# The first feed-forward fed from unscaled, turned rows, with the norm's root applied to every product tile

## The reference, cut to what matters

```python
x = x + rms_norm(merged @ w_out, norm_g[1])
h = rms_norm(x, norm_g[2])
gt, up = jnp.split(h @ w_ffn_in, 2, axis=-1)
x = x + rms_norm((jax.nn.silu(gt) * up) @ w_ffn_out, norm_g[3])
```

## Time and profile before

| | |
|---|---|
| median of 3 runs | 2281.73 us (2281.44 to 2281.91) |
| profiled execution, its own time | 2282.81 us |
| its span | 2281.0 us |
| PE busy, share of the span | 98% |
| DVE, ACT, POOL busy | 64%, 41%, 12% |
| mean granted clock of PE | 0.995 |
| DMA | 358 MB, 157 GB/s |

### The profile page before, as it was taken

One profiled execution on the slowest core, in us unless ns is written; L12 is line 12 of the kernel. 1 busy time (PEld: TensorE's weight loads), 2 busy tenths in 40 slices (PEclk: granted clock), 3 DMA queues, 4 the chain that ended last, 5 costly groups with the idle time before them and its releaser, 6 DMA issues.

```text
span 2281.0 us, 33428 instructions
## 1 busy us (share of the span) xinstructions
PE 2246.4 (98%) x14230; PEld 1963.7 (86%) x14230; DVE 1455.3 (64%) x1953; ACT 927.2 (41%) x1332; POOL 281.9 (12%) x254
## 2 busy tenths in 40 slices
PE   8999999999999999999999999999999999999999
PEld 8999986989998888888769888888888888988999
DVE  7675557777768767757858676326755332887554
ACT  7854447454562122235554212124322212556443
POOL 2020105111101011000110201000100101202111
PEclk9999989999999999999999999999999999999999
DMA  7453451746545444423204444223453321623443
GB/s 292 185 203 148 146 219 41 270 185 258 195 144 217 171 198 190 170 83 130 79 24 162 175 194 185 74 93 140 156 221 152 143 94 73 175 103 111 185 185 111
DMA packets 35728, 358.23 MB, mean 157 GB/s; under 512 B 4237, under 2 KB 6477, under 8 KB 9212
## 3 DMA queue, kind: packets, MB, share of 16 engines
q1 hardware_dynamic: 32124, 343.54, 39.6%
q0 software_dynamic: 3456, 12.56, 2.0%
HBM read 353.11 MB, written 1.13 MB: 155 GB/s over the span
## 4 chain that ended last, share of the span: by engine, by line
PE 93%; DVE 3%; ACT 2%; issue 1%; DMA 0%; SPq 0%; POOLq 0%; ACTq 0%; DVEq 0%
PE psum L931 25%; PE psum L932 25%; PE psum L933 25%; PE psum L1013 2%; PE psum L1012 2%; PE psum L1011 2%; PE psum L1324 1%; PE psum L952 1%; PE psum L947 1%; PE psum L948 1%; PE psum L1298 1%; PE psum L1253 1%; PE psum L1268 1%; DVE small L2798 0%; ACT arena_r L1631 0%
## 5 line engine op out<-in xcount | busy, mean ns | idle before, releaser
L931 PE MATMUL psum<-arena_r 128*128 128x256 f32 (+1 forms) x3096 | 1046.2, 338 | 5.2 <-DVE arena_r L2544 3.2
L933 PE MATMUL psum<-arena_r,ring_r 128*128 128x256 f32 (+1 forms) x3096 | 1039.8, 336 | 0.0
L932 PE MATMUL psum<-zT_r,arena_r 128*128 128x256 f32 (+1 forms) x2336 | 774.9, 332 | 0.0
L1631 ACT ACTIVATE arena_r<-ring 128x2048 fp32r<-128x2048 f32 (+1 forms) x252 | 473.4, 1880 | 691.0 <-PE psum L933 639.1
L2243 DVE TENSOR_TENSOR ring_r<-ring,arena_r 128x2048 fp32r<-128x2048 f32 (+1 forms) x252 | 572.3, 2273 | 192.5 <-ACT arena_r L1631 191.8
L931 PEld LDWEIGHTS psum<-arena_r 128*128 128x128 f32 x3096 | 583.8, 189 | 81.7 <-issue 4.7
L933 PEld LDWEIGHTS psum<-arena_r,ring_r 128*128 128x128 f32 x3096 | 586.4, 189 | 65.3
L932 PEld LDWEIGHTS psum<-zT_r,arena_r 128*128 128x128 f32 x2336 | 440.0, 188 | 43.8
L932 PE MATMUL psum<-arena_r 128*128 128x256 f32 (+2 forms) x1208 | 396.8, 328 | 0.0
L2399 DVE CUSTOM_DVE_ANT_0 psum<-arena,cb 128x1024 f32<-128x1024 f32 x256 | 318.0, 1301 | 0.0
L932 PEld LDWEIGHTS psum<-arena_r 128*128 128x128 f32 x1208 | 228.3, 189 | 22.1
(11 more groups left out here) (366 smaller groups left out, 2370.5 us busy)
## 6 DMA issues: line engine op xcount, KB each, us to landing
ring<-in_wf SPq DMA_DIRECT2D x75, 2048.0 KB, 7.5
ring<-in_w SPq DMA_DIRECT2D x40, 2048.0 KB, 7.6
arena<-in_w SPq DMA_DIRECT2D x73, 1024.0 KB, 9.4
ring<-in_wf SPq DMA_DIRECT2D x10, 1536.0 KB, 6.3
ring<-in_w SPq DMA_DIRECT2D x6, 1024.0 KB, 8.8
arena<-strip_scratch POOLq DMA_DIRECT2D x1, 2048.0 KB, 11.6
arena<-rpb_scratch POOLq DMA_DIRECT2D x16, 128.0 KB, 10.8
xT<-in_x SPq DMA_DIRECT2D x1, 1024.0 KB, 7.2
```

The lines of the kernel that those rows point to most:

```text
L931: mm(b[c][:, at], whc, xh[:, k, at], start=(k == ks[0]), stop=False)
L932: mm(b[c][:, at], whc, xl[:, k, at], start=False, stop=False)
L933: last = mm(b[c][:, at], wlc, xh[:, k, at], start=False, stop=(k == ks[-1]))
L1631: A(W_hi[h % NHI][:, 0:n], ring[:, half_slot(h)], ACT.Identity).then_inc(sig("w_hi"), 1)
```

## The change

It takes out the scaled tokens: the hi and lo parts are made of the turned x times the norm's weights, straight from PSUM, and the root is multiplied into both product tiles of every input half. So:

- **Border, by token tile.** DVE: sum, root, reciprocal and row additions of tile 0, then of tile 1 (`tile_rows`), each with its own root on ACT (`tile_root`); the weight rest that stood ahead of them is cut in two, one half ahead and one behind (`w_lo_part`). PE turns tile 0's rows, then tile 1's (`turn_rows_by_tile`). ACT squares the rows (`tile_squares`) and then writes the eight hi parts from PSUM (`raw_hi`); DVE writes the rests from PSUM (`raw_low`). The copies `x_back(0, ..)`, the scalings and the old parts are gone. The matmul that spreads the root moves in between the first half's matmuls, ahead of k = 3 (`raw_ready`), and ACT copies it to `R_root`.
- **Every input half of ffn 0.** DVE multiplies both tiles by `R_root` into `R_t` (`raw_half`) and signals with an empty instruction; ACT applies Silu in place (`raw_silu`); DVE multiplies gate and up (`raw_gate`, one half later, and the last of a group in the first output half); `a_high` also waits for that. Both tiles are now emptied by DVE.

The diff, cut to its core:

```diff
@@ make_plan @@
-                      "VV" if f == 4 and c == 0 else "AV")
+                      "VV" if f == 0 or f == 4 and c == 0 else "AV")
...
-    add("norm2", None, "V")
+    add("norm2", None, "A")
@@ tensor @@
+            def raw_ready(k):
+                pe.wait_ge(sig("raw_lo"), k + 1)
+                if k == 3:
+                    b = open_tile(TILE["norm2"])
+                    pe.wait_ge(sig("x_diag"), 1)
+                    mm(b[:, 0:S], C("ones"), rr[:, 0:2 * P], start=True, stop=True).then_inc(filled, 1)
...
+                    elif f == 0 and not second:
+                        split_part(h, half_banks(h), slice(0, S), R_hi, R_lo, filled,
+                                   before=raw_ready if i == 0 else None, both=i == 0)
...
-            turn_rows(0)
-            b = open_tile(TILE["norm2"])
-            pe.wait_ge(sig("x_diag"), 1)
-            mm(b[:, 0:S], C("ones"), rr[:, 0:2 * P], start=True, stop=True).then_inc(filled, 1)
+            turn_rows_by_tile()
@@ scalar @@
                     w_hi(h + 2)
+                    if f == 0 and not second:
+                        raw_silu(GROUPS[g][0] + j)
+                        if j > 0:
+                            a_high(g, j - 1)
...
+            def raw_silu(m):
+                act.wait_ge(sig("raw_t"), m + 1)
+                t = R_t[m % 2][:, 0, :]
+                A(t, t, ACT.Silu).then_inc(sig("raw_silu"), 1)
...
             evac_pairs("w_out", 4, w_out)
-            row_roots(0)
-            z_high(2, 0, 0, 2)
-            x_back(0, 3)
-            z_high(2, 0, 2, KT)
+            tile_squares()
+            raw_hi(0)
+            raw_hi(1)
+            act.wait_ge(sig("tok_sum"), 3)
+            A(X_RT, X_TOT, ACT.Sqrt, scale=1.0 / D, bias=C("eps")).then_inc(sig("tok_rt"), 1)
+            for k in range(2, KT):
+                raw_hi(k)
+            b = empty(TILE["norm2"])
+            A(R_root, b[:, 0:S], ACT.Identity).then_inc(evac["A"], 1)
@@ vector @@
+                    if f == 0 and second and j == 0:
+                        raw_gate(GROUPS[g][0] + GROUPS[g][1] - 1, GROUPS[g][1] - 1)
                     w_lo(h + 2)
+                    if f == 0 and not second:
+                        raw_half(m, n)
+                        if j > 0:
+                            raw_gate(m - 1, j - 1)
...
+            def raw_half(m, n):
+                if m == 0:
+                    wait_evac(dve, TILE["norm2"])
+                for i in range(2):
+                    b = empty(n + i)
+                    last = v.tensor_tensor(out=R_t[m % 2][:, i, :], in0=b[:, 0:S], in1=R_root, op=ALU.mult)
+                    last.then_inc(evac["V"], 1)
+                dve.engine_nop().then_inc(sig("raw_t"), 1)
+
+            def raw_gate(m, j):
+                dve.wait_ge(sig("raw_silu"), m + 1)
+                if m >= 2:
+                    dve.wait_ge(sig("a_lo"), m - 1)
+                t = R_t[m % 2]
+                v.tensor_tensor(out=(rt, rr)[j % 2][:, 0:S], in0=t[:, 1, :], in1=t[:, 0, :], op=ALU.mult)\
+                    .then_inc(sig("raw_gate"), 1)
...
+            gained(2, 0)
+            gained(2, 1)
+            w_lo_part(HALF_AT["w_out3"] + 2, 0)
             dve.wait_ge(sig("x_tok_in"), 16)
+            tile_rows(0, lambda: gained(3, 0))
+            tile_rows(1, lambda: gained(3, 1))
+            w_lo_part(HALF_AT["w_out3"] + 2, 1)
+            dve.wait_ge(sig("norm_sq"), 3 * KT)
+            v.tensor_reduce(out=X_TOT, in_=X_SUM.rearrange("p (t c) -> p t c", t=2), axis=AX, op=ALU.add)\
+                .then_inc(sig("tok_sum"), 1)
+            raw_low(0)
+            raw_low(1)
```

More of the change, by code:

```diff
@@ L967, in tail, with turn_rows_by_tile @@
                 split_part(h + 1, [high_bank(n + 2), high_bank(n + 3)], c_, xh, xl, filled, ks=ks)
+            def turn_rows_by_tile():
+                for t in range(2):
+                    for c in range(4):
+                        pe.wait_ge(sig("norm_x"), 4 * t + (2 if c < 2 else 4))
+                        for i in range(2):
+                            at = (4 + c) * BANK + i * S + t * P
+                            last = nc.tensor.transpose(psum[:, at:at + P], X_row[:, 4 * t + c, i * P:(i + 1) * P],
+                                                       C("ident"))
+                        if t == 1:
+                            last.then_inc(sig("x_turned"), 1)
             def turn_rows(n):
@@ L1055, in ffn @@
                     before = None
-                    if i == (2 if f == 4 else 0):
+                    if f == 4 and i == 2:
                         before = split_ready(NORM_BEFORE[f], 0)
@@ L1066, in ffn @@
                     else:
-                        split_features(h, nt, *((hi, lo) if second else (z_hi(nt), z_lo)), before=before,
-                                       both=i == (2 if f == 4 else 0))
+                        split_features(h, nt, *((hi, lo) if second else (z_hi(nt), z_lo)), before=before)
                     if f == 0 and i == CTX_TOTAL:
@@ L1772, in x_back, with tile_root, tile_squares, raw_hi @@
                   ACT.Identity).then_inc(sig("x_back"), 1)
+            def tile_root(t):
+                act.wait_ge(sig("tok_sum"), t + 1)
+                A(O_RT[:, t:t + 1], O_TOT[:, t:t + 1], ACT.Sqrt, scale=1.0 / D, bias=C("eps")).then_inc(sig("tok_rt"), 1)
+            def tile_squares():
+                for t in range(2):
+                    for h in range(2):
+                        k = 4 * t + 2 * h
+                        act.wait_ge(sig("norm_x"), k + 2)
+                        A(zT[:, k:k + 2, 0:S], X_row[:, k:k + 2, :], ACT.Square,
+                          accum_out=X_SUM[:, 2 * t + h:2 * t + h + 1]).then_inc(sig("norm_sq"), 2)
+            def raw_hi(k):
+                act.wait_ge(sig("x_turned"), k // 2 + 1)
+                A(R_hi[:, k, :], x_bank(k), ACT.Identity, scale=V("norm_g", 16 + k, 1)).then_inc(sig("raw_hi"), 1)
+            def raw_silu(m):
+                act.wait_ge(sig("raw_t"), m + 1)
+                t = R_t[m % 2][:, 0, :]
+                A(t, t, ACT.Silu).then_inc(sig("raw_silu"), 1)
             def row_roots(n):
-                act.wait_ge(sig("tok_sum"), 2 * n + 1)
+                act.wait_ge(sig("tok_sum"), 2 * n + 2)
                 A(O_RT, O_TOT, ACT.Sqrt, scale=1.0 / D, bias=C("eps")).then_inc(sig("tok_rt"), 1)
@@ L2490, in gained_out, with w_lo_part @@
                                        in1=G_row[3][:, c * S:(c + 1) * S], op=ALU.mult)
+            def w_lo_part(h, s):
+                n = HALVES[h][2] // 2
+                at = half_slot(h).start + s * n
+                if s == 0:
+                    assert h == lo_made[0]
+                    dve.wait_ge(sig("w_hi"), h + 1)
+                low = v.tensor_tensor(out=ring_r[:, at:at + n], in0=ring[:, at:at + n],
+                                      in1=W_hi[h % NHI][:, s * n:(s + 1) * n].bitcast(f32), op=ALU.subtract)
+                if s == 1:
+                    lo_made[0] += 1
+                    low.then_inc(sig("w_lo"), 1)
@@ new lines, in raw_low @@
+            def raw_low(k):
+                dve.wait_ge(sig("raw_hi"), 2 * (k // 2) + 2)
+                v.scalar_tensor_tensor(out=R_lo[:, k, :], in0=x_bank(k), scalar=V("norm_g", 16 + k, 1),
+                                       in1=R_hi[:, k, :].bitcast(f32), op0=ALU.mult, op1=ALU.subtract)\
+                    .then_inc(sig("raw_lo"), 1)
+            def raw_half(m, n):
+                if m == 0:
+                    wait_evac(dve, TILE["norm2"])
+                for i in range(2):
+                    b = empty(n + i)
+                    last = v.tensor_tensor(out=R_t[m % 2][:, i, :], in0=b[:, 0:S], in1=R_root, op=ALU.mult)
+                    last.then_inc(evac["V"], 1)
+                dve.engine_nop().then_inc(sig("raw_t"), 1)
@@ new lines, in raw_gate, with tile_rows @@
+            def raw_gate(m, j):
[5 more added lines that the diff above has]
+                    .then_inc(sig("raw_gate"), 1)
+            def tile_rows(t, between):
+                dve.wait_ge(sig("norm_sq"), KT + 7 + t)
+                v.tensor_reduce(out=O_TOT[:, t:t + 1], in_=O_SUM[:, 4 * t:4 * t + 4], axis=AX, op=ALU.add)\
+                    .then_inc(sig("tok_sum"), 1)
+                link(between())
+                dve.wait_ge(sig("tok_rt"), t + 1)
+                link(v.reciprocal(O_RR[:, t:t + 1], O_RT[:, t:t + 1]))
+                for h in range(2):
+                    k = slice(4 * t + 2 * h, 4 * t + 2 * h + 2)
+                    v.scalar_tensor_tensor(out=X_row[:, k, :], in0=Y_y[:, k, :], scalar=O_RR[:, t:t + 1],
+                                           in1=xT[:, k, 0:S], op0=ALU.mult, op1=ALU.add).then_inc(sig("norm_x"), 2)
@@ L2918, in _ @@
             dve.wait_ge(sig("g_row_in"), 2 * 16)
-            for c in range(4):
+            for c in range(3):
                 lo(f"w_out{c}")
@@ L2925, in _ @@
                     gained(c - 1, 1)
[L2926 removed]
```

(14 more changed lines are left out.)

41 lines of the change are left out of this document (19 added, 22 removed).

## The result

| | before | after |
|---|---|---|
| median | 2281.59 us (2278.72 to 2282.80, 6 runs) | 2291.78 us (2287.98 to 2294.72, 6 runs) |
| profiled execution, own time and span | 2282.81, 2281.0 | 2294.01, 2292.2 |
| ratio to before | | 1.005 (95% interval 1.004 to 1.006) |

The change makes the kernel slower by 10.2 us in the medians (9 to 14 by the interval). 2293 was forecast.

What follows compares the result with a forecast made beforehand. The prediction took PE, busy for 98% of the span, as the bound. Feed-forward waits of 13.75 us less 2.7 us gained at the border, +11.1 on the 2281.73 us median, made 2293 us; 8-in-10 range 2286 to 2300.

Steps and rivals of the forecast that it cites:

- The ring: First feed-forward's input halves: split, DVE work, Silu and copy wait in a loop, 5.7 us a round against PE's 5.65.
- lag of a set of dots: Input halves: four adaptation reduces on DVE delay the emptying of a half's tiles by 2.9 us per set.
- Waits per group: First feed-forward: PE waits 3.75, 8.75 and 1.25 us in groups 0, 1 and 2, 13.75 us together.
- lag - 1.55: PE's wait per group, early waits for empty tiles included: the accumulated delay less 1.55 us of slack.
- POOL's last subtraction: At each group's end, ahead of the first output half: taken at 1.1 us, some 1 us lower sum if short.
- The border: Output projection to first feed-forward: first matmul 3.9 us earlier, less 1.2 for the root's matmuls, a gain of 2.7.
- The root's matmuls: Two matmuls moved from the border into the first input half, charged 1.2 us there at the low clock.
- With the low clock as before: Behind the border: PE's clock falls as in the old kernel, so the gain there is 2.7 us.
- rival 2: At the border the clock stays up: 2.2 us off, 2290.8 us; chance 0.12.
- Rival 1: New feed-forward waits make the clock fall again, about 2.4 us each: 2295.4 or 2297.8 us; chance 0.21.
- Sum: Whole kernel: 13.75 us of waits less 2.7 gained at the border, +11.1 us, giving 2293 us.
- rival 3: Feed-forward loop has slack: 2284 to 2287 us (chance 0.07), or only the border's gain, 2279.0 or 2276.8 (0.06).

Runs made afterwards that it cites:

- ring_alone: Changed kernel with adaptation dots cut to 8 columns (results left out) and context squares moved to output halves 8 to 11; ratio 0.9986 to the kernel before.
- short_dots: Changed kernel with the adaptation dots of halves 2 to 17 cut from 1024 columns to 8, results left out; 2279.4 us, ratio 0.9992 to the kernel before.
- early_squares: Changed kernel with the context squares and their sums moved from halves 12 to 19 to output halves 8 to 11; 2288.8 us, ratio 1.0036 to the kernel before.
- open_ring: Changed kernel with ACT's order altered: Silu and copy taken one half later, behind the next split; 2278.0 us, ratio 0.9983 to the kernel before.
- open_early_squares: Changed kernel with Silu and copy one half later and context squares in output halves 8 to 11; ratio 0.9985 to the kernel before.
- open_early_again: The same program as open_early_squares, run and profiled a second time; 2275.32 us, ratio 0.9984 to the kernel before.
- open_filled: open_early_squares plus 4, 5 and 9 identity turns on PE in the border's three gaps; 2274.65 us, ratio 0.9977 to the kernel before.
- copy_beside: Changed kernel with ACT's copy taken one half later, behind the next split and ahead of Silu; 2291.2 us, ratio 1.0044 to the kernel before.

## Why the prediction was right, point by point

The forecast, 2293, was 1.2 us from the median, and the mechanism was the one named: a ring without slack that pays for every side task. That the number came so close is luck. It missed 4.5 us of cost (1.5 in the delays, 3.0 of low clock) and 3.5 us of gain at the border, and the two cancelled.

- **The ring** was right: 5.7 us a round was expected, 5.65 came (5.655 in ring_alone, 5.27 without the copy). The lag of a set of dots was 2.75, expected 2.9. That nothing is made up is shown by the splits; that the dots and squares carry the cost, by short_dots and early_squares; that the order does, by open_ring.
- **Waits per group** were expected at 3.75, 8.75 and 1.25; the delays were 4.9, 9.1 and 1.3. Sum 15.3 for 13.75. The term "lag - 1.55" left out that each stop costs about 0.25 beside its wait, and it had the last product of group 1 free of the context sum, which held it up by some 1 us (open_ring against open_early_squares).
- **POOL's last subtraction**, taken at 1.1, was 0.73 (the median of both groups of rows is 0.738, the longest 1.08):

```profile
L838 POOL TENSOR_TENSOR arena_r<-rt,arena_r x11: 725/738/1081, 476.8 to 652.9; 128x256 fp32r<-128x256 f32 x11
```

  The range of the earlier trace rows, 0.74 to 1.61, has shrunk: the subtraction now mostly falls where DVE stands and waits for ACT's split. By the rule of the Trainium skill's page "SBUF — State Buffer", section "Who interferes with whom", a POOL instruction beside an idle DVE is the undisturbed one; the trace agrees with 0.73 there. DVE's second reduce, which ran beside a 1.08 one, took 1.77 and not 1.26.
- **The border**: first matmul 3.9 earlier expected, 3.97 measured. The root's matmuls were charged 1.2 at the low clock: 1.19 is how long the two took in the view, and not by how much the next is pushed back, which is 0.24, and 0.5 where the clock was low (short_dots). "With the low clock as before" failed in the profiled run; there rival 2 held, worth 2.5 where 2.2 was priced. So the border gave 6.2 and not 2.7.
- **Rival 1** held as well, in group 1: one fall of 3.0 us where 2.4 was priced. It fell at the place named, but not in group 0, where waits of 1.4 and 2.7 us left the clock at 1.00.
- **Sum**: 13.75 - 2.7 = 11.05 expected; 15.3 + 3.0 - 6.2 = 12.1 in the profiled pair and 10.2 in the medians. Of the ten profiles with this border the clock stayed up in five, so "as before" and "up" can both come true; 0.12 for rival 2 was too little.
- **Not slower** (rival 3) failed, because the ring has no slack. Only the border's gain would have made 2276.8 with the clock up, as the rival priced it; open_early_again measured 2275.3 and open_filled 2274.7, with a kernel before at 2279.7.

What stays open: what decides the clock's fall. In group 0 the change stood 1.4 and 2.7 us and kept the clock; early_squares stood 0.9 and 2.7 there and lost it, and copy_beside lost it after 1.2 and 0.8. These runs don't tell why.

## What to carry to other kernels

Before an operation is put behind another engine's work, write down the loop of waits through all engines and the one instruction of each that stands in program order, and compare its sum with the bounding engine's round: at equality it costs nothing, but any work that comes now and then on one of these engines is then paid in full, until the loop opens. Take the consumer one round later (here Silu and copy behind the next split, no buffer more), and keep side work from standing ahead of the last product of a group. Judge a change of some tenths of a per cent by the length of its stage in the trace, between two landmarks, when the code ahead of it varies by more than the change.

## What was not expected of the hardware

- The clock at the border isn't reproducible. Ten profiles have the same border (eight turns, a gap, eight turns, gaps of 0.6, 0.9 and 1.5 us), and their programs differ only behind it: five kept 1.00, and five fell, four of them for 3.0 us of loss and one for 1.5. The one program that was profiled twice fell both times, once for each of these.
- A run's time goes with its mean clock, but the border is the smaller part of that. open_early_again's runs were 2273.5 to 2274.2 at a mean clock of 0.998 to 0.999, and 2279.4 to 2280.3 at 0.996. Yet open_filled, whose profile (2277.5) had the clock at 1.00 over the whole stage, ran at 2272.6 to 2272.7 (0.999) and at 2277.4 to 2277.6 (0.997) as well. Over the profiles the stretch between 315 and 350 us loses 1.7 to 6.8 us and the border 0 to 3.0.
- Shorter waits did not mean less low clock. copy_beside had 5.1 us less of waits than the change and 1.9 us more of low clock, with three falls. The Trainium skill's page "TensorE: Matmul & The Clock Gate", section "HAM oscillation — how this bites in real kernels", tells of a loop that pays the low clock behind each of its waits; here it was paid in copy_beside behind waits of 1.2 and 0.8 us (low from 513), and not behind those of 1.4 and 2.7 in group 0 of the change.
